# Sliding-window attention: the two half-filled key blocks of a head packed into one

## The reference

```python
# WINDOW = ATTN_BLOCK = 128, 16 query heads, 4 key/value heads, head size 64
kk, vv = with_prev(kb), with_prev(vb)          # the block before and the own block: 256 keys
s = einsum('bnqhgd,bnkhd->bnhgqk', qb, kk) * hd ** -0.5
dist = ATTN_BLOCK + arange(128)[:, None] - arange(256)[None, :]
mask = (dist >= 0) & (dist < WINDOW)           # and no block before the first
s = where(mask, s, -inf)
m = maximum(max(s), sink)
p = exp(s - m)
o = einsum('bnhgqk,bnkhd->bnqhgd', p / (sum(p) + exp(sink - m)), vv)
```

## Time and profile before

| what | value |
|---|---|
| median of 3 runs | 1833.17 us (1831.25 to 1833.58) |
| profiled execution, own time | 1830.42 us |
| its span, first to last instruction | 1828.6 us |
| PE busy | 1793.6 us, 98% |
| DVE, ACT, POOL busy | 1287.4 (70%), 987.2 (54%), 536.7 us (29%) |
| busy from 284 to 534 us, attention of segment 1: PE, DVE, ACT, POOL | 248.01, 179.53, 195.07, 167.81 us |
| the same from 1023 to 1273 us, segment 2 | 247.92, 178.50, 195.17, 167.40 us |
| granted TensorE clock | 0.998 of full speed |

### The profile page before, as it was taken

How to read it: one execution, slowest core, us unless ns; L and a number is a source line. 1 busy time by engine, 2 the same in 40 slices (tenths; PEclk the granted TensorE clock), 3 DMA queues, 4 the chain that set the end, 5 groups by cost and what they waited for, 6 DMA issues and landing times.

```text
span 1828.6 us, 29466 instructions
## 1 busy us (share of the span) xinstructions
PE 1793.6 (98%) x10368; PEld 1504.6 (82%) x10368; DVE 1287.4 (70%) x2628; ACT 987.2 (54%) x2127; POOL 536.7 (29%) x857
## 2 busy tenths in 40 slices
PE   6899999999999999999999999999999999999999
PEld 4788888888878888888888888887888887888887
DVE  7966467777766566697546677776776557987987
ACT  5622226777776665662222577777655555343341
POOL 1000026777733223310002567773333321000000
PEclk9999999999999999999999999999999999999999
DMA  9243232221222344344233222121433148278252
GB/s 356 70 161 108 100 118 89 76 74 53 69 96 93 110 143 126 102 167 161 81 121 110 101 75 74 39 82 54 161 93 88 63 134 292 105 253 304 93 179 92
DMA packets 158497, 222.36 MB, mean 122 GB/s; under 512 B 11792, under 2 KB 104336, under 8 KB 150672
## 3 DMA queue, kind: packets, MB, share of 16 engines
q1 hardware_dynamic: 158352, 220.49, 36.2%
HBM read 163.18 MB, written 57.28 MB: 121 GB/s over the span
## 4 chain that ended last, share of the span: by engine, by line
PE 90%; issue 3%; DVE 2%; ACT 2%; POOL 2%; DMA 1%; SPq 0%; DVEq 0%; POOLq 0%; ACTq 0%
PE bank L898 70%; PE bank L1055 3%; PE bank L1044 3%; PE bank L1076 3%; PE bank L1137 2%; PE bank L1124 2%; PE bank L1109 2%; PE bank L1102 1%; PE bank L1008 1%; DMA h_f<-x_cols 1%; PE bank L1151 1%; PE bank L1126 1%; PE bank L1093 0%; DMA raw<-in_w_in 0%; PE bank L1011 0%
## 5 line engine op out<-in xcount | busy, mean ns | idle before, releaser
L898 PE MATMUL bank<-h_hi,w_hi 128*128 128x512 f32 x512 | 206.5, 403 | 0.2
L898 PE MATMUL bank<-h_lo,w_hi 128*128 128x512 f32 x512 | 199.9, 390 | 0.0
L898 PE MATMUL bank<-h_hi,w_lo 128*128 128x512 f32 x512 | 199.7, 390 | 0.0
L898 PE MATMUL bank<-wq_hi,h_hi 128*128 128x384 f32 x512 | 177.0, 346 | 0.5 <-issue 0.5
L898 PE MATMUL bank<-ob_hi,oa_hi 128*128 128x512 f32 x448 | 175.0, 391 | 0.0
L898 PE MATMUL bank<-ob_lo,oa_hi 128*128 128x512 f32 x448 | 174.4, 389 | 0.0
L898 PE MATMUL bank<-ob_hi,oa_lo 128*128 128x512 f32 x448 | 174.3, 389 | 0.0
L898 PE MATMUL bank<-wq_hi,h_lo 128*128 128x384 f32 x512 | 172.0, 336 | 0.0
L898 PE MATMUL bank<-wq_lo,h_hi 128*128 128x384 f32 x512 | 171.3, 334 | 0.0
L1319 ACT ACTIVATE g_hi<-g_raw 128x2048 fp32r<-128x2048 f32 x36 | 69.0, 1917 | 163.5 <-PE bank L898 155.4
L1477 ACT ACTIVATE sm<-sm,neg_m 128x257 f32<-128x257 f32 x256 | 127.4, 504 | 18.0 <-DVE neg_m L2043 17.9
(11 more groups left out here) (255 smaller groups left out, 4834.8 us busy)
## 6 DMA issues: line engine op xcount, KB each, us to landing
g_raw<-in_w_in SPq DMA_DIRECT2D x24, 1024.0 KB, 6.2
raw<-in_w_in SPq DMA_DIRECT2D x16, 1024.0 KB, 8.5
o_lower<-mixed_cols SPq DMA_DIRECT2D x32, 512.0 KB, 6.2
nat_rows<-u SPq DMA_DIRECT2D x48, 256.0 KB, 2.6
raw<-in_w_in SPq DMA_DIRECT2D x8, 1536.0 KB, 6.7
o_upper<-in_w_out SPq DMA_DIRECT2D x24, 512.0 KB, 8.1
wa<-in_w_ada SPq DMA_DIRECT2D x8, 1024.0 KB, 11.6
g_q<-gate_cols SPq DMA_DIRECT2D x64, 128.0 KB, 2.5
```

The costliest lines, as they stand in the source:

```text
L898: mm = pe.matmul(dst, a, b, start=(first and m == 0), stop=(last and m == 2), **more)
```

## The change

The scores of both key blocks are still made (256 columns a head). Then the two halves are packed: ACT copies the 128 columns of the block before to `sm` (two instructions for four heads; in the first block of the sequence it copies a constant of -1e30 instead), and DVE lays the own block's score over it where `own` (k <= q) is one, by a predicated copy a head. The maximum is one reduction over the four heads. Exponentials, normalising and transposes work on 128 columns a head; four transposes fill one bank, 5 or 6 by turns, which ACT alone copies to `pT`. DVE multiplies `pT` by `prev_T` (k > q), giving `pTm`, and makes `vd`, v of the block before less v of the own block; the product is v times `pT` plus `vd` times `pTm`, in four matmuls as before.

The order on the engines changes too. On ACT the copy of `pT` goes ahead of the normalising (and, in step 35, ahead of the recurrence's first `decays`). On DVE `qn` goes ahead of the packing and the maximum, and `o_mix` (now `mix_out`) behind them, one step later: block `b-6` in step `b`, until steps 34 to 36 catch up. The transposes no longer wait for the copies of the block just ahead, but for those two blocks ahead.

```diff
@@ -526,8 +528,8 @@
...
-            for dst, src in ((masks[:], masks_d), (causal[:], causal_d)):
-                sp.dma_start(dst, src).then_inc(late_in, 16)
+            for dst, src in ((own[:], own_d), (prev_T[:], prev_d), (causal[:], causal_d)):
+                sp.dma_start(dst, src).then_inc(const_in, 16)
...
@@ -1035,14 +1037,10 @@
                 if 4 <= b <= ATT_B + 3:
                     j = b - 4
                     pe.wait_ge(pn_ok, S + j + 1)
-                    if j >= 1:
-                        pe.wait_ge(pta_ok, S + j)
-                        pe.wait_ge(ptv_ok, S + j)
+                    if j >= 2:
+                        pe.wait_ge(pta_ok, S + j - 1)
                     for h in range(GH):
-                        for half in range(2):
-                            at = ((h % 2) * 2 + half) * P
-                            mm = pe.transpose(bank[5 + h // 2][:, at:at + P],
-                                              sm[j % 2][:, h, half * P:(half + 1) * P], ident[:])
+                        mm = pe.transpose(bank[5 + j % 2][:, h * P:(h + 1) * P], sm[j % 2][:, h, 0:P], ident[:])
                     mm.then_inc(pt_ok, 1)
...
@@ -1050,10 +1048,10 @@
                     pe.wait_ge(ptv_ok, S + j + 1)
                     if j >= 1:
                         pe.wait_ge(omix_ok, S + j)
-                    for half in range(2):
+                    for v, p_T in ((vv[:, j % NBLK + 1, :], pT), (vd[:, j % NBLK, :], pTm)):
                         for e in range(2):
-                            mm = pe.matmul(bank[7][e * HD:(e + 1) * HD, 0:2 * P], vv[:, j % NBLK + half, :],
-                                           pT[j % 2][:, e:GH:2, half, :], start=(half == 0), stop=(half == 1))
+                            mm = pe.matmul(bank[7][e * HD:(e + 1) * HD, 0:2 * P], v, p_T[j % 2][:, e:GH:2, :],
+                                           start=(p_T is pT), stop=(p_T is pTm))
                     mm.then_inc(pv_ok, 1)
...
@@ -1064,7 +1062,7 @@
...
-                        pe.wait_ge(masked_ok, (GH + 1) * (S + j))
+                        pe.wait_ge(own_ok, (GH + 2) * (S + j))
...
@@ -1444,6 +1442,19 @@
 
             def att_iter(s, b):
                 S = s * ATT_B
+                if 3 <= b <= ATT_B + 2:
+                    j = b - 3
+                    act.wait_ge(s_ok, S + j + 1)
+                    if j >= 2:
+                        act.wait_ge(pt_ok, S + j - 1)
+                    first = s == 0 and j % NBLK == 0
+                    if first:
+                        act.wait_ge(const_ok, 4)
+                    for e in range(2):
+                        src = bank[2 + e][:, :].rearrange("p (a c) -> p a c", a=2)[:, :, 0:P]
+                        act.activation(sm[j % 2][:, e:GH:2, 0:P],
+                                       no_prev[:].unsqueeze(1).to_broadcast([P, 2, P]) if first else src, ACT.Copy
+                                       ).then_inc(prev_ok, 1)
                 if b == ATT_B + 1:
                     act.wait_ge(krot_ok, S + ATT_B)
                     forget_tanh(s, 0)
@@ -1474,7 +1485,7 @@
...
-                        act.activation(sm[j % 2][:, h, 0:2 * P + 1], sm[j % 2][:, h, 0:2 * P + 1], ACT.Exp,
+                        act.activation(sm[j % 2][:, h, 0:P + 1], sm[j % 2][:, h, 0:P + 1], ACT.Exp,
...
@@ -1489,22 +1500,22 @@
...
                 if 4 <= b <= ATT_B + 3:
                     j = b - 4
                     act.wait_ge(pt_ok, S + j + 1)
                     if j >= 2:
                         act.wait_ge(pv_ok, S + j - 1)
-                    act.activation(pT[j % 2][:, 0:2, :, :].rearrange("p h a q -> p (h a q)"), bank[5][:, :],
-                                   ACT.Copy).then_inc(pta_ok, 1)
+                    act.activation(pT[j % 2][:].rearrange("p h q -> p (h q)"), bank[5 + j % 2][:, :], ACT.Copy
+                                   ).then_inc(pta_ok, 1)
+                if 3 <= b <= ATT_B + 2:
+                    j = b - 3
+                    act.wait_ge(rden_ok, S + j + 1)
+                    for h in range(GH):
+                        a = act.activation(sm[j % 2][:, h, 0:P], sm[j % 2][:, h, 0:P], ACT.Identity,
+                                           scale=r_den[j % 2][:, h:h + 1])
+                    a.then_inc(pn_ok, 1)
+                if b == ATT_B + 3:
+                    decays(s, 0)
...
@@ -2020,28 +2031,20 @@
...
+            def mix_out(s, j):
+
+                S = s * ATT_B
+                dve.wait_ge(pv_ok, S + j + 1)
+                dve.wait_ge(gs_ok, S + j + 1)
+                if j >= 2:
+                    dve.wait_ge(att_out[j % 2], 16 * ((S + j) // 2))
+                for t in range(2):
+                    a = dve.scalar_tensor_tensor(o_mix[j % 2][:, t, :], bank[7][:, t * P:(t + 1) * P], 0.5,
+                                                 g_q[j % 4][:, t, :], ALU.mult, ALU.mult)
+                a.then_inc(omix_ok, 1)
+
             def att_iter(s, b):
...
@@ -2052,6 +2055,33 @@
                     dve.tensor_tensor(qn[:], bank[j % 2][:, 0:QW + HD].rearrange("p (h d) -> p h d", d=HD),
                                       q_rinv.unsqueeze(2).to_broadcast([P, GH + 1, HD]),
                                       ALU.mult).then_inc(qn_ok, 1)
+                if 3 <= b <= ATT_B + 2:
+                    j = b - 3
+                    waits = [(prev_ok, 2 * (S + j + 1))]
+                    if j >= 1:
+                        waits.append((max_ok, S + j))
+                    if j >= 2:
+                        waits.append((pt_ok, S + j - 1))
+                    waits_alone(dve, *waits)
+                    sinks_at = slice(j // NBLK * GH, (j // NBLK + 1) * GH)
+                    dve.tensor_copy(sm[j % 2][:, :, P:P + 1], sink_bc[:, sinks_at].unsqueeze(2)).then_inc(own_ok, 1)
+                    for h in range(GH):
+                        at = (h // 2) * 2 * P + P
+                        dve.copy_predicated(sm[j % 2][:, h, 0:P], own[:], bank[2 + h % 2][:, at:at + P]).then_inc(own_ok, 1)
+                    dve.wait_ge(own_ok, (GH + 2) * (S + j) + GH + 1)
+                    dve.reduce_max(row_max, sm[j % 2][:, :, 0:P], AX_X).then_inc(own_ok, 1)
+                    dve.wait_ge(own_ok, (GH + 2) * (S + j + 1))
+                    dve.scalar_tensor_tensor(neg_m[j % 2], row_max, -1.0, sink_neg[:, sinks_at],
+                                             ALU.mult, ALU.min).then_inc(max_ok, 1)
+                if 6 <= b <= ATT_B + 2:
+                    mix_out(s, b - 6)
+                if 1 <= b <= ATT_B:
+                    j = b - 1
+                    if s > 0 and j % NBLK == 0:
+                        dve.wait_ge(carry_in, 48 * (j // NBLK + 1))
+                    if j >= NBLK:
+                        dve.wait_ge(pv_ok, S + j - NBLK + 1)
+                    dve.tensor_tensor(vd[:, j % NBLK, :], vv[:, j % NBLK, :], vv[:, j % NBLK + 1, :], ALU.subtract)
                 if b == 1:
                     rotate_first(s)
                 if 2 <= b <= ATT_B + 1:
@@ -2093,24 +2123,14 @@
...
                 if 4 <= b <= ATT_B + 3:
                     j = b - 4
-                    dve.wait_ge(pt_ok, S + j + 1)
-                    if j >= 2:
-                        dve.wait_ge(pv_ok, S + j - 1)
-                    dve.tensor_copy(pT[j % 2][:, 2:4, :, :].rearrange("p h a q -> p (h a q)"),
-                                    bank[6][:, :]).then_inc(ptv_ok, 1)
...
+                if b >= ATT_B + 2:
+                    mix_out(s, b - 5)
...
@@ -2401,7 +2421,8 @@
...
-                    dve.wait_ge(late_in, 32)
+                    dve.wait_ge(const_in, 16 * 11)
+                    dve.memset(no_prev[:], NEG)
...
@@ -2546,16 +2567,13 @@
...
-    prev = np.where(k > q, 0.0, NEG)
-    own = np.where(k <= q, 0.0, NEG)
-    first = np.concatenate([np.full((P, P), NEG), own], 1)
-    later = np.concatenate([prev, own], 1)
-    masks = np.stack([first, later], 1).astype(np.float32)
+    own = (k <= q).astype(np.int32)
+    prev_T = (q > k).astype(np.float32)
...
```

More of the change, by code:

```diff
@@ L200, in hybrid_layer @@
         q_ss, q_var, q_rinv = [named[n][:, 0:GH + 1] for n in ("q_ss", "q_var", "q_rinv")]
-        q_rot, k_rot, qT_hi, qT_lo, sm, pT, o_mix = [[named[f"{n}{i}"] for i in range(2)] for n in
-                                                     ("q_rot", "k_rot", "qT_hi", "qT_lo", "sm", "pT", "o_mix")]
+        vd = named["vd"]
+        q_rot, k_rot, qT_hi, qT_lo, sm, pT, pTm, o_mix = [[named[f"{n}{i}"] for i in range(2)] for n in
+                                                     ("q_rot", "k_rot", "qT_hi", "qT_lo", "sm", "pT", "pTm", "o_mix")]
         kT_hi, kT_lo, vv, no_key = [named[n] for n in ("kT_hi", "kT_lo", "vv", "no_key")]
@@ L1491, in att_iter @@
                     act.activation(vv[:, i + 1, :], bank[b % 2][:, QW + HD:QKV], ACT.Copy).then_inc(v_read, 1)
-                if 3 <= b <= ATT_B + 2:
-                    j = b - 3
-                    act.wait_ge(rden_ok, S + j + 1)
```

(10 more changed lines are left out.)

50 lines of the change are left out of this document (12 added, 38 removed).

## The result

The kernel after the change takes 1844.07 us (median of 5 runs, 1841.15 to 1844.26) where the kernel before takes 1831.91 (1829.71 to 1833.58): a ratio of 1.0058, 95% interval 1.0047 to 1.007. It is slower by 12 us. The forecast was 1830.7 with a range up to 1844.0; the time of the rival "the ring is longer than PE's block everywhere" (1844.5) is what came.

What follows compares the result with a forecast made beforehand. PE, busy 98%, was taken as the bound. On 1830.42 us, -29.1 (transposes) + 20.2 (stalls) + 6.4 (stage ends) = -2.5 gives 1827.9; the timed median stands 2.75 higher: 1830.7, range 1813 to 1844.

Steps and rivals of the forecast that it cites:

- the ring is longer than PE's block everywhere: Rival for the attention blocks: rings of 8.03 us with a weight split, 7.08 without; 1844.5 us, chance 0.24.
- Part 3: End of each attention stage: PE waits for the later o_mix and last product, costing 3.2 us a segment, 6.4 in both.
- Part 1: PE's attention blocks: four transposes fewer save 0.485 us a block, 7.46 to 6.98, over 60 blocks 29.1 us.
- Part 2: Attention blocks' round through DVE and POOL: it stalls PE 10.1 us a segment, 20.2 in both.
- PE bounds the kernel now, and the change's chain decides: Whole kernel: PE is busy 98%; in attention, the other engines' long chain decides, not their busy share.
- the ring: Attention-block cycle qn, masks, lows, q_ss, root, qn: 7.78 us with a weight split, 6.83 without, against PE's 6.98.
- pTm from 4.95, POOL's q_rinv held behind it: Block without a weight split: pTm starts 4.95 us after qn and delays POOL's q_rinv; next qn at 6.83.
- between runs 0.6 is won back: Blocks between runs of weight splits: DVE recovers 0.15 us in each of four, 0.6 in all.
- The late weights: Weight loads in later runs of splits land some 3.1 us late, lengthening the cycle 0.8 to 0.9 us once a run.
- PE stays the bound: Rival for the attention blocks: the cycle loses some 0.45 us, to 7.3 with a split; 1814.5 us, chance 0.27.
- nothing shed: Rival: the change doesn't shed what it says, PE's block stays at 7.46 us, the end costs 6.4; 1839.6, chance 0.04.

Runs made afterwards that it cites:

- Experiment 8: Changed kernel with pTm read from PSUM, o_mix back at the step's end and decays ahead of the last pT copy: 1809.21 us, ratio 0.9875.
- experiment 5: Changed kernel with idle matmuls on PE in the two long waits for o_mix at each attention stage's end: 1840.23 us, ratio 1.0044.
- experiment 4: Changed kernel with pTm reading the transposed probabilities from PSUM instead of SBUF, its place in the order kept: 1821.58 us, ratio 0.9947.
- experiment 7: Changed kernel with the packing kept but all orders of before (qn, o_mix, normalising, decays): 1829.96 us, ratio 0.9981.

## Why the prediction was wrong, step by step

The sum gave -2.5 us and the span grew by 13.7, so it missed by 16.2. The step that failed most is Part 3, the end of the stage, priced at 3.2 us a segment where 7.3 were measured (8.3 us in the run): it has no term for the matmul clock after a wait and none for pTm held by POOL's k_inv. Then come the size of Part 1 (4.0) and that of the stall in Part 2 (3.5), together 15.8; the other 0.4 us lie outside the attention stages and their ends.

*PE bounds the kernel now, and the change's chain decides.* Right: the loss is in waits of PE that weren't there, and busy shares moved by two points.

*Part 1, four transposes save 0.485 us.* A little too high. Experiment 8 shows PE alone: 0.97 to 0.53, and a block of 7.018 us in the mean against 7.465, so 0.447. That is worth 28 blocks of a segment, not 30: the stage of experiment 8 is 12.5 and 12.6 us shorter than before, where 14.55 was counted, so 4.0 us in the run. The price of four had been taken as half of eight; if each transpose costs the same, 0.97 and 0.53 give 0.11 for one and 0.09 beside, which stays.

*Part 2, the ring.* The ring exists as forecast, and qn waits for q_rinv in every block. Without a split it was forecast at 6.83 and is 7.12. The step that failed there is "pTm from 4.95, POOL's q_rinv held behind it": it is q_var that is held. q_rinv therefore starts 0.14 behind pTm's end instead of at it; the sum for a block with a split had this term, that for a block without one had not. q_ss and pTm come 0.13 us later than summed (5.08): neg_m, ahead of the exponentials, takes 0.33 us for 0.16 beside POOL's rc. The rest is 0.02. This small error has a large effect, since PE's own block (7.03) lies between the two numbers: "between runs 0.6 is won back" became nothing won back. With a split it was forecast at 7.78 and is 7.38: vd and g_q were taken at 0.28 and 0.58, as beside POOL's rotations, and take 0.13 and some 0.3 between starts. The late weights were right in kind and too small: issued 5.1 us later than in the earlier trace rows, where 3.6 had been worked out, and 1.2 us on the first block of a run (8.6 against 7.4), not 0.8 to 0.9. In sum the stall of the first segment is 227.28 - 216.99 = 10.3 us (10.1 forecast, where the terms as written give 10.3: 3 x 0.8 - 1.5 is 0.9 and not 0.7). That it fits is luck: the errors cancel. The blocks without a split lost 1.9 us of it, and 8.4 fell on the eleven in runs of splits. The stall of the second segment is 13.5: its first blocks lost 2.0 us, with a stretch of half clock at 1041.89, and one block took 12.79 us, since a load took 9.2 us to land where the median is 6.8, with half clock behind its wait. The two give 3.5 us over the forecast.

*Part 3, the end, 3.2 us a segment.* This is the largest error. The first product came where forecast (3.32 us behind the transposes; 3.3). To the 3.2 us come 1.7 us of half clock behind the first wait, 1.1 us for pTm held by k_inv, 0.8 us of half clock at the last product, 0.2 elsewhere, and 0.85 more in the projection behind it; 0.45 that the blocks ahead of it shed goes off. That is 7.3 us an end, 8.3 us in the run above the forecast. The split of the half clock is worked out from starts in the trace; experiment 5, which takes it away, gives 2 to 3 us an end for all of it. I priced the two waits, and not what a wait does to PE's clock afterwards. The page "TensorE: Matmul & The Clock Gate" of the Trainium skill ("Why this matters for your kernels") warns of idle gaps between bursts of matmuls. It would have added a rival, and experiment 5 agrees with it; the gaps that it names are longer than the 2.66 us behind which the clock fell here.

*The rival that came.* Its condition, a ring above PE's block without a split too, holds (7.12 over 7.03). Its price came close by chance: it had 17 us of stall a segment, measured are 10.3 and 13.5, and 3.2 an end, measured 7.3. Its ring with a split (8.03) was further off than the forecast's (7.78), at 7.38 measured. "PE stays the bound" is ruled out by the 64 waits of qn, "nothing shed" by experiment 8. The page "SBUF — State Buffer" of the Trainium skill ("Who interferes with whom") had the rule on which the ring rests, and experiment 4 agrees with it: the same operation with one operand in PSUM leaves POOL's 0.20 us alone. What the page states about the lock was used for q_rinv, and had to be applied to every pair: pTm with k_inv, rc with neg_m.

## What to carry to other kernels

When an engine at the bound sheds work, compare the other engines' ring with its new block, not the old one: here the ring stood 0.09 us above PE's block, which cost little by itself but left no slack, so that every longer block was lost in full; and an old order that fitted 7.46 us no longer fitted 7.03 (experiment 7). Where two SBUF operands on DVE lie beside a short POOL operation on the critical ring, read one operand from PSUM before moving instructions about; that edit alone took the ratio to before from 1.0058 to 0.9947, of 0.9875 for all three. At a stage's end price a wait of the matmul engine with what its clock does afterwards.
